# Layer passages of a hybrid block: x additions on VectorE through PSUM, two first units side by side, feature sums placed anew

## The reference, cut to what matters

```python
def rmsnorm_2(x, g):
    y = xf * lax.rsqrt(jnp.mean(xf * xf, axis=-1, keepdims=True) + RMS_EPS)
    return (y * g.astype(jnp.float32)).astype(x.dtype)

for i in range(DEPTH_2):
    m = fox_attention(hn, ...) if i % 2 == 0 else short_conv(hn, ...)
    x = x + rmsnorm_2(m, g[1])
    f = sq_relu_mlp(rmsnorm_2(x, g[2]), w_mlp_up[i], w_mlp_down[i])
    x = x + rmsnorm_2(f, g[3])
    gate = jax.nn.sigmoid(rmsnorm_2(x, g[4]) @ w_ple_gate[i])
    e = (p[i] @ w_ple_proj[i]) * gate
    x = x + rmsnorm_2(e, g[5])
```

## Time and profile before

| | |
|---|---|
| median of 3 runs | 1817.66 us |
| profiled execution | 1817.59 us, of which span 1815.8 us |
| PE busy | 1748.6 us (96%), mean granted clock 0.989 |
| DVE busy | 1069.6 us (59%) |
| ACT busy | 740.2 us (41%) |
| POOL busy | 180.0 us (10%) |
| chain that ended last | PE 71%, issue 13%, DVE 6%, POOL 5%, ACT 4%, DMA 2% |

### The profile page before, as it was taken

How to read it: one execution, slowest core, us unless ns; L and a number is a source line. 1 busy time by engine, 2 the same in 40 slices (tenths; PEclk the granted TensorE clock), 3 DMA queues, 4 the chain that set the end, 5 groups by cost and what they waited for, 6 DMA issues and landing times.

```text
span 1815.8 us, 21865 instructions
## 1 busy us (share of the span) xinstructions
PE 1748.6 (96%) x8300; PEld 1436.1 (79%) x8300; DVE 1069.6 (59%) x1397; ACT 740.2 (41%) x1076; POOL 180.0 (10%) x144
## 2 busy tenths in 40 slices
PE   8999999999899999999999999979998999999987
PEld 6978877888688887778888887758886888888866
DVE  6367767676556777573535354785557544444475
ACT  4256664665425666442212123542125222222245
POOL 2000110000300000320000002330004000000041
PEclk9999999999999999999999999989999999999999
DMA  7222123214233222132232321313322322233211
GB/s 243 91 69 69 38 65 100 68 50 139 70 82 93 70 71 65 58 116 93 93 96 99 106 93 58 118 56 98 111 82 70 116 93 93 92 96 100 94 62 55
DMA packets 164726, 160.36 MB, mean 88 GB/s; under 512 B 13881, under 2 KB 157526, under 8 KB 164390
## 3 DMA queue, kind: packets, MB, share of 16 engines
q1 hardware_dynamic: 164646, 159.26, 28.0%
HBM read 150.43 MB, written 4.19 MB: 85 GB/s over the span
## 4 chain that ended last, share of the span: by engine, by line
PE 71%; issue 13%; DVE 6%; POOL 5%; ACT 4%; DMA 2%; POOLq 0%; SPq 0%; DVEq 0%; ACTq 0%
PE bank L768 22%; PE bank L770 22%; PE bank L769 22%; POOL ssum L2430 3%; PE bank L1027 2%; PE bank L1045 1%; DVE split_weights L1761 1%; DVE work L1822 1%; POOL tmp L2463 1%; DVE act_a L1809 1%; ACT split_weights L1273 1%; DMA raw_weights<-in_w_mlp_up 1%; DMA raw_weights<-in_w_ple_gate 1%; ACT sq L1302 1%; POOL ssum L2434 1%
## 5 line engine op out<-in xcount | busy, mean ns | idle before, releaser
L768 PE MATMUL bank<-act_a,split_weights 128*128 128x512 f32 x1392 | 558.9, 402 | 26.9 <-DVE act_a L1809 26.4
L770 PE MATMUL bank<-act_a,split_weights 128*128 128x512 f32 x1392 | 546.6, 393 | 0.0
L769 PE MATMUL bank<-act_a,split_weights 128*128 128x512 f32 x1392 | 546.3, 392 | 0.0
L1273 ACT ACTIVATE split_weights<-raw_weights 128x2048 fp32r<-128x2048 f32 (+1 forms) x118 | 221.7, 1879 | 336.4 <-PE bank L770 336.4
L1761 DVE TENSOR_TENSOR split_weights<-raw_weights,split_weights 128x2048 fp32r<-128x2048 f32 (+1 forms) x118 | 273.4, 2317 | 123.2 <-ACT split_weights L1273 119.8
L768 PEld LDWEIGHTS bank<-act_a,split_weights 128*128 128x128 f32 x1392 | 263.7, 189 | 90.4 <-issue 23.0
L770 PEld LDWEIGHTS bank<-act_a,split_weights 128*128 128x128 f32 x1392 | 263.0, 189 | 57.5
L769 PEld LDWEIGHTS bank<-act_a,split_weights 128*128 128x128 f32 x1392 | 263.7, 189 | 53.5 <-issue 2.2
L768 PE MATMUL bank<-act_b,split_weights 128*128 128x512 f32 x664 | 260.4, 392 | 0.0
L769 PE MATMUL bank<-act_b,split_weights 128*128 128x512 f32 x664 | 258.4, 389 | 0.0
L770 PE MATMUL bank<-act_b,split_weights 128*128 128x512 f32 x664 | 258.4, 389 | 0.0
(11 more groups left out here) (192 smaller groups left out, 2052.1 us busy)
## 6 DMA issues: line engine op xcount, KB each, us to landing
raw_weights<-in_w_mlp_up SPq DMA_DIRECT2D x32, 1024.0 KB, 5.4
raw_weights<-in_w_mlp_down SPq DMA_DIRECT2D x32, 1024.0 KB, 5.1
raw_weights<-in_w_in SPq DMA_DIRECT2D x20, 1024.0 KB, 5.3
raw_weights<-in_w_conv_in SPq DMA_DIRECT2D x12, 1024.0 KB, 5.1
raw_weights<-in_w_attn_in SPq DMA_DIRECT2D x16, 512.0 KB, 4.6
raw_weights<-in_w_ple_gate SPq DMA_DIRECT2D x8, 1024.0 KB, 5.1
raw_weights<-in_w_out SPq DMA_DIRECT2D x4, 1024.0 KB, 5.2
raw_weights<-in_w_attn_in SPq DMA_DIRECT2D x4, 1024.0 KB, 5.2
```

Of the source, the lines that this page charges most:

```text
L768: nc.tensor.matmul(dst, w[0], a[0], start=first, stop=False)
L769: nc.tensor.matmul(dst, w[0], a[1], start=False, stop=False)
L770: mm = nc.tensor.matmul(dst, w[1], a[0], start=False, stop=last)
L1273: nc.scalar.activation(wsp[:, pl.slot, 0, pl.split_cols], raw[:, pl.slot, pl.raw_cols], ACT.Copy)\
```

## The change

Names that are used below: `banks[SCALED + k % 2]` is bank4 and bank5 by turns, and line numbers in the pieces of order are those of the changed kernel where the piece is of it.

- **Additions.** m writes its product into bank4 or bank5, and reads rstd from bank7, where ACT now leaves it; a reads that bank and x from SBUF, and all eight additions stand on DVE. POOL has only its sums.
- **Orders.** DVE, ACT and the final norm have new orders; the second half of the weight splits stands earlier.
- **First units.** The two first units run side by side over k = 0 to 4, then unit 0 over 5 to 7, then unit 1 over 5 to 7, with the sum for the new rstd behind k = 5 of unit 1 (12 matmuls follow). `opening_units` keeps the old order for the first projection of all.
- **Feature sums.** `begin_statistics` stands behind the last unit, `end_statistics` ahead of the embedding projection.
- **fox_qk.** Its unit 1 is split by halves, the first half ahead of rstd.
- **Fox mask.** The mask's matmul is the last of the three.

```diff
-        FOX_ORDER = "h0 u1 h1 h2 q0 h3 q1 h4 q2 h5 q3 h6 q4 h7 q5 q6 q7"
-        HI_ORDER = "h0 h1 e0 h2 h3 w0 q0 q1 h4 w1 h5 q2 q3 h6 q4 h7 q5 q6 q7"
+        FOX_ORDER = "h0 h1 q0 h2 w1 q1 h3 q2 h4 q3 h5 q4 h6 q5 h7 q6 q7"
+        HI_ORDER = "h0 e0 h1 q0 w0 h2 q1 w1 h3 q2 q3 h4 q4 h5 q5 h6 q6 h7 q7"
-        POOL_ADDS = range(1, 4)
-        NORM_ORDER = "m0 a0 m1 m2 l0 m3 l1 m4 l2 a4 l3 w0 m5 a5 l4 m6 a6 l5 m7 a7 l6 l7 w1"
+        NORM_ORDER = "m0 a0 m1 l0 a1 m2 l1 a2 m3 l2 a3 w0 m4 l3 a4 w1 m5 l4 a5 m6 l5 a6 m7 l6 a7 l7"
+        FINAL_ORDER = "m0 m1 l0 m2 l1 m3 l2 w1 m4 l3 m5 l4 m6 l5 m7 l6 l7"
...
+        BOTH = 5
+        FIRST_UNITS = [(u, k) for k in range(BOTH) for u in (0, 1)] + [(u, k) for u in (0, 1) for k in range(BOTH, KT)]
+        SUM_BEFORE = (1, KT - 2)
+        SCALED = 4
...
-                    if late and (k, m) == order[-2]:
-                        late()
...
+                for u, k in FIRST_UNITS:
+                    pl = units[u]
+                    if (u, k) == SUM_BEFORE:
+                        statistics(KT)
+                    if k == 0 and u in halved:
+                        pe.wait_ge(half_split, halves if u == 0 else halves - len(halved) + 1)
+                    if k == (KT // 2 if u in halved else 0):
+                        pe.wait_ge(w_split, pl.u + 1)
...
+                    if u == 0:
+                        pe.wait_ge(in_ready, ready + k + 1)
+                    first_tiles(pl, k)
...
                         part(0, 2, P, first=True)
+                        part(1, 3, P, last=True)
                         nc.tensor.matmul(dst[:, j * P:(j + 1) * P], identb[:, :], maskb[:, MASK["fox"], :],
-                                         start=False, stop=False)
-                        part(1, 3, P, last=True).then_inc(A["scores"], 1)
+                                         start=False, stop=True, skip_group_check=True).then_inc(A["scores"], 1)
...
+                end_statistics()
                 for m in range(4):
-                    if m == 1:
-                        end_statistics()
...
+            split_half("fox_qk", 1, 0)
-            make_rstd(rstd[:, :], D)
+            make_rstd(banks[7][:, :], D)
...
                 def scale(k):
-                    m = wt(tiles_at + k)
-                    V.scalar_tensor_tensor(out=m, in0=m, scalar=col(gain + k), in1=rstd[:, :], op0=ALU.mult, op1=ALU.mult)\
-                        .then_inc(out_scaled, 1)
+                    V.scalar_tensor_tensor(out=banks[SCALED + k % 2][:, :], in0=wt(tiles_at + k), scalar=col(gain + k),
+                                           in1=banks[7][:, :], op0=ALU.mult, op1=ALU.mult).then_inc(out_scaled, 1)
 
                 def add(k):
...
-                    V.tensor_tensor(wt(X + k), wt(X + k), wt(tiles_at + k), ALU.add).then_inc(x_ready, 1)
+                    V.tensor_tensor(wt(X + k), banks[SCALED + k % 2][:, :], wt(X + k), ALU.add).then_inc(x_ready, 1)
...
-                for k in POOL_ADDS:
-                    pool.wait_ge(out_scaled, n["scaled"] + k + 1)
-                    pool.wait_ge(x_ready, n["x"] + KT + k)
-                    nc.gpsimd.tensor_tensor(wt(X + k), wt(X + k), wt(tiles_at + k), ALU.add).then_inc(x_ready, 1)
```

79 lines of the change are left out of this document (39 added, 40 removed).

## The result

| | before | changed kernel |
|---|---|---|
| median of the runs | 1817.71 us (1817.23 to 1817.77, 4 runs) | 1804.26 us (1802.81 to 1805.36, 4 runs) |
| profiled execution (span) | 1817.59 (1815.8) | 1803.77 (1802.0) |

The ratio is 0.9926, with a 95% interval of 0.9909 to 0.9943. The forecast was 1799.6 us: direction right, 1804.26 inside the range, 0.3 us outside the forecast's own range of 1796 to 1804. The change brings 13.5 us where 18.0 were expected. So both are to be explained: what came, and the 4 to 5 us that did not.

A forecast was written before the change was run, and what follows sets the result against it. PE, busy 96%, loses time waiting for low parts and POOL's last sum, with DVE behind both. Gains of 9.9 + 3.6 + 3.0 + 1.5 = 18.0 us from 1817.59 gave 1799.6 us; own range 1796 to 1804, with rivals 1791 to 1811.

The forecast's parts named there:

- The bound: In the layer passages PE loses 5.2 us waiting for low parts and POOL's last sum and at the lower clock.
- DVE's list: Projection passages: 18.4 us of DVE work plus 4.2 of hold by POOL's seven sums; l7 ends 22.6 us behind m0.
- What POOL holds: Beside POOL's sums only l and weight halves are held, not m and a: 0.6 us per sum, 4.2 a passage.
- The first rival: Lock covers m and a too: each of POOL's seven sums costs 1.0 us, 13.6 in all, 1813.2 us; 15%.
- The rival at 1804.6: Touching PSUM costs up to 0.06 us extra per m and a, 5 us in five passages; 12%.
- The new wait: From l7 through the third unit's weight split 6.7 us: third unit at 29.3 behind m0, gain 3.3, three times.
- PE alone bounds: Rival: POOL's sums fall between low parts, l7 never late, third unit at 27.2 us; 26.4 us gained, 1791.2; 15%.
- m into PSUM is long: Rival: m writing bank4 while bank7 is read takes 1.76 us, 27 us net in five passages, about 1843; 4%.
- the idle time now lies ahead of the feature sum, where it costs nothing: Projection passages: idle time moved ahead of the feature sum is free, since the square was awaited anyway.
- A lower clock early on would be absorbed there, so I count none: PE's first units: needing a tile each 2.7 us, they absorb an early lower clock; counted as no cost.
- fox_qk 1.5 us: fox_qk's passage: drain spared 0.9 us, start to wf 24.9 against 25.6; gain 1.5 us, between 0 and 2.
- The Fox mask at nothing: Fox attention: the same three matmuls with the short one last gain nothing; bounds 7.7 us less or more.

The follow-up runs named there:

- the experiment with short sums: Copy-first kernel with six of POOL's seven running sums cut to 64 of 512 columns, the rest left out: 1788.41 us, one run.
- with everything in SBUF: Copy-first kernel with m written in place and rstd in SBUF, all additions still on DVE: 1816.52 us, 21.2 us above copy-first.
- copy-first: Changed kernel with DVE copying (or adding) the last tile out of PSUM before splitting the weight half, no longer behind it: 1795.34 us, ratio 0.9876.
- the run with four parts: Changed kernel with unit 0 then unit 1 over k = 0 to 3, then again over 4 to 7: 1811.46 us, ratio 0.9963.
- the fastest version: Copy-first kernel with the last feature sum behind the projection's first tile again: 1792.85 us, ratio 0.9866.

## Why the prediction was right, and where it failed

**The bound: right.** Behind m0 the first units waited for their input and the row sum for POOL. The first wait fell from 26.4 to 14.3 us, the second from 5.4 to 0.3. The last low part itself came no earlier (22.64 against 22.69 us behind m0): as the forecast counted it, what is spared is PE's work behind it and the wait for POOL.

**DVE's list: right in its sum, wrong in its parts.** l7 was put at 22.6 us behind m0 and came at 22.64. The terms were 18.4 of own work and 4.2 of POOL's hold. The trace has 1.8 us of lengthened instructions (two weight halves by 0.5, two l by 0.4), and the experiment with short sums bears that out: 1.25 for six of the seven, 0.5 for the first. About 2.3 us of gaps in which l waits for ACT's high part (0.52, 0.71, 0.79 in three of the rows) were not in the sum. Two errors cancelled, which is luck. A row of idle time ahead of an l could not be read before the change, but ACT's list could have been added up as DVE's was.

**What POOL holds: right.** m and a were taken as not held up, and are not: 0.74 and 0.68 inside a POOL sum. The first rival, the lock over m and a, is excluded by these rows. Its price was too small: with everything in SBUF it is 21.2 us, where 13.6 had been worked out. In that trace six DVE instructions of mlp0's passage are 1.0 to 1.1 us longer, 6.3 us in all, near the 7.0 that the rival had for seven hits. What was off is the sum that it was set against, 4.2 us where 1.8 were measured: the difference is 4.5 us a passage, not 2.8. The Trainium skill (SBUF — State Buffer, "SBUF: two separate sides") ties the exclusive port to DVE instructions with two SBUF inputs; the traces agree, for a PSUM output too, with 1.77 against 0.74 us for the same m.

**No surcharge for PSUM.** m is 0.74 to 0.76 us with rstd and product in banks and 0.75 with both in SBUF; a is 0.68 and 0.69. The rival at 1804.6 lies nearest to the measured 1804.26 by its number, but its mechanism is absent. The Trainium skill (VectorE: DVE Perf Modes, "The TRN2 errata") has a larger fixed cost for a PSUM source; no row here shows it.

**The new wait: right, but only just.** Where the projection runs at the full clock, the passage is as forecast: 29.5 us from m0 to the third unit in mlp0 and ple_gate0 against 29.3, 29.2 in ple_gate1 against 29.0. conv_in, without a projection, has 28.65 against 28.4. The third unit waits 0.17 us for the first read with the new rstd, behind the split, and the rstd sum no longer waits for POOL. So PE's own work behind the last low part is only 0.17 us shorter than DVE's way through the split: a faster split would bring no more than that. "PE alone bounds" is excluded, since PE waits for l7 (0.48 us), which that rival had never late; "m into PSUM is long" by m's 0.74.

**"the idle time now lies ahead of the feature sum, where it costs nothing": failed.** m0 did not move, which is what the step argued from. But the projection's first tile now stands behind m0. ACT, which copies the projection's tiles out of PSUM between its high parts, waits for them twice (0.76 us each, at 763.63 the second), so h2 starts 4.64 us behind m0 and not 3.66, and l2, l7 and the rstd sum follow almost 1 us later: four times 0.95, 3.8 us, as the experiment with the sums in their old places shows. That PE starts the first units at 3.94 instead of 3.17 us is not what costs, as PE waits for l7 in both. The forecast had l7 at 22.6 for another reason, so these 3.8 us are no part of the 4 to 5 that are missing from it; they are what the kernel could have had besides.

**"A lower clock early on would be absorbed there, so I count none": failed.** PE now idles 1.85 to 2.30 us ahead of the last feature sum in the four passages with a projection, against 0.4 to 0.9 before. In mlp1 the profile shows what follows: L904 takes 1.61 us, and the matmuls behind it stand 0.43 us apart, the lower of the two levels (1.2 instead of 2.4 GHz). L904 is on the chain to rstd and the projection is ahead of PE's start, so neither is absorbed: 0.5 us before m0 and 1.1 behind it, which is mlp1's 1.6 against 3.2 elsewhere. The kernel run again has it in two passages, and its runs spread over 5.5 us. With the idle time down to 0.85 us or less, in the copy-first kernels and with the sums in their old places, no such matmul is seen ahead of these first units, and the runs of each lie within 0.35 to 2.7 us. That the clock makes the spread is likely and not shown, as only one run of each has a trace. conv_in has it too: its last sum takes 1.39 us after 1.98 us of idle time, where before it took 1.12 after the same 1.98, about 0.3 of the 0.5 us that are missing there. That the chip falls to the lower level in some executions after this idle time and not in others, is seen; what decides it is not.

**fox_qk 1.5 us: half, and again the clock.** The 0.9 of the drain came as 0.7. The 0.6 of the shorter start did not come: from m0 to wf it is 28.06 us against 28.07. PE starts at 2.50 us as before, after an idle 3.85 us, but with twelve matmuls 0.43 us apart, where before there were nine and the forecast counted nine: three times 0.2 us. The kernel with the sums in their old places has nine, and 24.86 us from PE's start to wf, where 24.9 had been forecast. The work was counted rightly; how many matmuls run slow differs from execution to execution, from nine to fourteen in these traces.

**The last stage: not forecast.** PE's second group of transposes waits 0.75 us for ACT's copy out of a bank, and the last sum runs at the lower clock, 1.80 us where it took 1.05. The wait and the slower transposes behind it are 0.9 us, the last sum 0.75: most of the 1.9 us given back. The wait is also in the copy-first kernel (0.73), and it is gone where only the order of the first units is the old one, in the run with four parts:

```profile
1779.80 1.47 PE L1253 MATMUL bank<-consts,work 128*128 128x128 f32 x12
```

So it is the price of the side-by-side order in this stage. The slow last sum is not: it lasts 1.05 us, as before, in the fastest version.

**The Fox mask at nothing: small, but wrong.** It is worth 0.4 us by the trace, far within the bounds of 7.7. The other 1.1 us of this stretch are the clock in the last pair of heads, which was at the lower level before the change and is not after it. Nothing in the forecast spoke for that, so for its number this is luck.

By the sum, then: 18.0 forecast; fox_qk -0.8, the mask and last pair +1.5, mlp1 -1.7, the other four passages -1.3, the last stage -1.9. That makes 13.8, the difference of the two profiled executions. By cause: the lower clock took 0.6 us in fox_qk, 1.6 in mlp1, 0.3 in conv_in and 0.75 in the last sum, and was absent from Fox's last pair, which gave 1.1; the transposes' wait took 0.9, the mask gave 0.4, and the 1.5 us that remain are 0.1 to 0.4 in each of seven stretches. What the forecast counted as work came out within a few tenths in every passage; what it put at nothing, as absorbed, was the clock.

## What to carry to other kernels

When an instruction is moved off a wait "because the wait ends later anyway", ask what the waiting engine did meanwhile: the work that filled the gap is now behind it, and an idle TensorE may come back at its lower clock just where the chain runs. Where a copy only has to free or square a tile, let it go ahead of weight work that hangs on a transfer: one call, moved behind the copy in two places, gave 8 us here. Where DVE and POOL both work on SBUF, route one operand of each DVE instruction through a free PSUM bank: 21 us of 1795 here, for no cost in the instruction itself. And before a difference of a microsecond between two traces is put down to an edit, look at the granted clock of that stretch.

## What the runs showed of the hardware

- A DVE product or sum of 128x512 fp32 takes the same time with one operand in PSUM, and with a PSUM output, as wholly in SBUF (0.74 to 0.76 and 0.68 to 0.69 us). Beside a POOL addition in SBUF it is held to as much as 1.74 to 1.78 us if both inputs are in SBUF; none of the 40 products and 40 sums with one input in PSUM was held (0.68 to 0.76 us).
- POOL's own addition of 1.33 us grows to 1.47 and 1.55 beside DVE, so both pay.
- After 1.7 to 2.3 us of idle time TensorE was granted the lower clock in some executions and not in others: behind the same 1.7 to 1.8 us in Fox's last pair in four traces of thirteen, at 1.06 us each, and not in the nine others. The runs of the kernel with about 2 us of idle time in five passages spread over 5.5 us, those of its copy-first version, with 0.68 us in four of them, over 0.35.
- Putting the short bf16 matmul last of three instead of between two passes gave 0.07 us for each of six pairs of heads.
